# Norms, layer norms and residual sums of a two-model transformer kernel: VectorE's signals carried by its instructions, and one rounding moved to ScalarE

## The reference

```
# first block, each of two layers (x: 512 tokens, s_c: 256 context tokens)
hx = rms_norm(x, norm1_g) * (1 + mod[1]) + mod[0]
x  = x + mod[2] * mixer(hx)                       # mLSTM + convolution, then attention
x  = x + mod[5] * sqrelu_mlp(rms_norm(x, norm2_g) * (1 + mod[4]) + mod[3])

# second block, each of two layers
h = x @ w_in                                      # queries, keys, values and gates of 3 branches
merged = (g[:, :, 0] * (o_mla  @ wb[:MLA_OUT]) + g[:, :, 1] * (o_diff @ wb[MLA_OUT:...])
          + g[:, :, 2] * (o_mem @ wb[...:]))      # g = sigmoid(gates)
x = layernorm(ALPHA * x + merged @ w_out, ln1_g, ln1_b)
f = square(relu(x @ mlp_w1)) @ mlp_w2
x = layernorm(ALPHA * x + f, ln2_g, ln2_b)
```

## Time and profile before

| | |
|---|---|
| time, median of 3 runs | 4470.93 us (4465.73 to 4476.07) |
| time of the profiled execution | 4468.7 us |
| its span, first to last instruction | 4465.8 us |
| mean granted TensorE clock | 0.939 |
| PE busy | 4019.3 us, 90% |
| DVE busy | 2118.9 us, 47% |
| ACT busy | 1495.7 us, 33% |
| POOL busy | 1641.7 us, 37% |

### The profile page before, as it was taken

The page is one execution under the profiler, slowest core; times in us unless marked ns, Lnnn a source line. Parts: engine busy times, 40 slices in busy tenths (PEclk is TensorE's granted clock), DMA queues, the critical chain, the costliest instruction groups (busy, mean ns, idle before and its releaser), DMA issues.

```text
span 4465.8 us, 62758 instructions
## 1 busy us (share of the span) xinstructions
PE 4019.3 (90%) x20662; PEld 3353.9 (75%) x20662; DVE 2118.9 (47%) x3412; ACT 1495.7 (33%) x2419; POOL 1641.7 (37%) x2044
## 2 busy tenths in 40 slices
PE   4887788999988888999999999899988999998997
PEld 3776677999987766888777678688866767876885
DVE  5455464333245776334655632533357376235235
ACT  3111122111124553222545543222236355323223
POOL 0111112333331103666333345356632433544564
PEclk6888898999998999999999999899989999998998
DMA  3232211111111001222211122222211211222222
GB/s 138 101 122 98 106 62 43 62 62 62 63 55 34 20 15 55 97 96 94 67 57 62 53 76 91 71 85 96 97 64 37 76 53 53 96 84 67 98 94 85
DMA packets 92786, 328.64 MB, mean 74 GB/s; under 512 B 10240, under 2 KB 12544, under 8 KB 92544
## 3 DMA queue, kind: packets, MB, share of 16 engines
q1 hardware_dynamic: 90928, 323.61, 21.8%
q10 hardware_dynamic: 1616, 1.90, 0.1%
HBM read 323.38 MB, written 2.10 MB: 73 GB/s over the span
## 4 chain that ended last, share of the span: by engine, by line
issue 67%; POOL 33%; POOLq 1%
POOL Wl L264 33%; POOLq L259 0%; POOLq L261 0%; POOLq L264 0%; POOLq L147 0%; POOLq L258 0%; POOLq L3288 0%
## 5 line engine op out<-in xcount | busy, mean ns | idle before, releaser
L264 POOL TENSOR_TENSOR Wl<-raw,Wh 128x256 fp32r<-128x256 f32 x2040 | 1641.5, 835 | 2823.5 <-ACT Wh L371 2823.4
L371 ACT ACTIVATE Wh<-raw 128x1024 fp32r<-128x1024 f32 x510 | 540.2, 1059 | 1924.1 <-PE psum L1095 1684.6
L1093 PE MATMUL psum<-Hh,Wh 128*128 128x512 f32 (+1 forms) x2704 | 1052.8, 389 | 95.7 <-DVEq L1945 59.9
L1094 PE MATMUL psum<-Hl,Wh 128*128 128x512 f32 (+1 forms) x2704 | 1026.3, 380 | 0.0
L1095 PE MATMUL psum<-Hh,Wl 128*128 128x512 f32 (+1 forms) x2704 | 1025.4, 379 | 0.0
L1093 PE MATMUL psum<-Gh,Wh 128*128 128x512 f32 (+3 forms) x2032 | 756.0, 372 | 31.3 <-DVEq L1945 27.5
L1095 PE MATMUL psum<-Gh,Wl 128*128 128x512 f32 (+3 forms) x2032 | 747.6, 368 | 0.0
L1094 PE MATMUL psum<-Gl,Wh 128*128 128x512 f32 (+3 forms) x2032 | 747.0, 368 | 0.0
L1093 PEld LDWEIGHTS psum<-Hh,Wh 128*128 128x128 f32 x2704 | 525.2, 194 | 230.2 <-DVEq L1945 67.1
L1095 PEld LDWEIGHTS psum<-Hh,Wl 128*128 128x128 f32 x2704 | 525.1, 194 | 72.4
L1094 PEld LDWEIGHTS psum<-Hl,Wh 128*128 128x128 f32 x2704 | 527.1, 195 | 66.0 <-issue 1.3
(11 more groups left out here) (336 smaller groups left out, 4740.2 us busy)
## 6 DMA issues: line engine op xcount, KB each, us to landing
raw<-in_wstream SPq DMA_DIRECT2D x510, 512.0 KB, 3.3
stage<-in_ada SPq DMA_DIRECT2D x80, 512.0 KB, 4.1
M<-in_ada SPq DMA_DIRECT2D x16, 512.0 KB, 4.7
X<-in_xT SPq DMA_DIRECT2D x1, 2048.0 KB, 12.8
out<-X SPq DMA_DIRECT2D x8, 256.0 KB, 2.0
X<-in_ctxT SPq DMA_DIRECT2D x1, 1024.0 KB, 7.8
M<-in_memT ACTq DMA_DIRECT2D x1, 1024.0 KB, 6.1
M<-in_axial ACTq DMA_DIRECT2D x1, 512.0 KB, 3.5
```

The source lines that it names most:

```text
L264: last = pool.tensor_tensor(Wl[:, s, c], raw[:, s, c], Wh[:, s, c].bitcast(F32), ALU.subtract)
L371: act.activation(Wh[:, s], raw[:, s], ACT.Copy).then_inc(v["w_high"], 1)
L1093: pe.matmul(dst, a[0], b[0], start=first, stop=False)
L1094: pe.matmul(dst, a[0], b[1], start=False, stop=False)
```

## The change

1. **Signals by the instruction.** In `rms` the two pieces of `T(k)`, and the two of `Hl(k)`, follow each other without a wait; the signal to ScalarE is raised by the last piece of `T(k)` itself. In `layer_norm` `T(k)` raises `for_act` and `Hl(k)` raises `for_pe` itself (all but the last), with no wait on the chain behind them. In `centred_sums` the subtraction of the early mean raises `for_act` itself. In `add_gated` the addition raises `bank_free` itself, except where the sum is read next (`followed=True`), where nothing changes but the call. In `hidden` the signal to TensorE stands ahead of the one that gives ScalarE's slot back.
2. **The sum of branches.** ScalarE rounds `M` to `Gh` (`high_sums`), VectorE only subtracts (`low_sums`) and signals TensorE by the subtraction itself. Rows 4 and 5 are done inside the third branch, between its steps m = 4 and m = 6; the other six behind it. The projection takes the rows in the order 4, 5, 0, 1, 2, 3, 6, 7 for its first and all further tiles.

```diff
+OUT_ORDER = (4, 5, 0, 1, 2, 3, 6, 7)
...
@@ ScalarE, second_act @@
+    def high_sums(ms):
+
+        act.wait_ge(v["for_act"], wants.next())
+        for m in ms:
+            act.activation(v["Gh"][:, m, X0:TOK], v["M"][:, m * SEQ:(m + 1) * SEQ], ACT.Copy).then_inc(v["high_done"], 1)
+
     def branch(i, paired, begun):
 
         for m in range(0, KT, 2):
+            if i == 2 and m == 6:
+                high_sums(OUT_ORDER[:2])
             if m or not begun:
...
     branch(2, True, True)
+    high_sums(OUT_ORDER[2:])
...
@@ TensorE @@
-                project(w, slice(0, P), G, X0, SEQ, per_k=1 if m == 0 else 0)
+                project(w, slice(0, P), G, X0, SEQ, per_k=1 if m == 0 else 0, ks=OUT_ORDER)
...
@@ VectorE, rms @@
-                        stt(T[k % 3][:, lo:hi], X[:, k, lo:hi], A[:, 8 * c + k:8 * c + k + 1], psum[:, 5 - c, 0:hi - lo],
-                            ALU.mult, ALU.mult)
-                    for_act()
+                        last = dve.scalar_tensor_tensor(out=T[k % 3][:, lo:hi], in0=X[:, k, lo:hi], scalar=A[:, 8 * c + k:8 * c + k + 1],
+                                                        in1=psum[:, 5 - c, 0:hi - lo], op0=ALU.mult, op1=ALU.mult)
+                    last.then_inc(v["for_act"], 1)
...
+                        last = dve.scalar_tensor_tensor(out=Hl[:, k - 2, lo:hi], in0=T[(k - 2) % 3][:, lo:hi],
+                                                        scalar=mod[:, 6 * layer + shift, k - 2, c:c + 1],
+                                                        in1=Hh[:, k - 2, lo:hi].bitcast(F32), op0=ALU.add, op1=ALU.subtract)
+                    do(last)
                     for_pe()
...
@@ VectorE, centred_sums @@
-                tt(x(k), x(k), psum[:, 5, :], ALU.subtract)
-                for_act()
+                dve.tensor_tensor(x(k), x(k), psum[:, 5, :], ALU.subtract).then_inc(v["for_act"], 1)
...
@@ VectorE, layer_norm @@
-                    stt(T[k % 4], x(k), lvec[:, gcol + k:gcol + k + 1], psum[:, 4, :], ALU.mult, ALU.mult)
-                    for_act()
+                    dve.scalar_tensor_tensor(out=T[k % 4], in0=x(k), scalar=lvec[:, gcol + k:gcol + k + 1], in1=psum[:, 4, :],
+                                             op0=ALU.mult, op1=ALU.mult).then_inc(v["for_act"], 1)
...
+                    if k < KT + 1:
+                        last.then_inc(v["for_pe"], 1)
+                    else:
+                        do(last)
+                        for_pe()
...
@@ VectorE, add_gated @@
+                if followed and t0 + n == TOK:
+                    do(last)
+                    free(b)
+                else:
+                    last.then_inc(v["bank_free"][b], 1)
...
@@ VectorE, hidden @@
-                    split(Gh[:, m, t0:t0 + w], Gl[:, m, t0:t0 + w], r)
+                    cp(Gh[:, m, t0:t0 + w], r)
+                    do(dve.tensor_tensor(Gl[:, m, t0:t0 + w], r, Gh[:, m, t0:t0 + w].bitcast(F32), ALU.subtract))
+                    for_pe()
                     give_back()
-                    for_pe()
...
@@ VectorE, sum of branches @@
+            def low_sums(ms):
+
+                for m in ms:
+                    dve.wait_ge(v["high_done"], diff_counts.high_done.next())
+                    dve.tensor_tensor(Gl[:, m, X0:TOK], M[:, m * SEQ:(m + 1) * SEQ], Gh[:, m, X0:TOK].bitcast(F32),
+                                      ALU.subtract).then_inc(v["for_pe"], 1)
+
...
+                    if n == 2 and m == 4:
+                        for_act()
+                        low_sums(OUT_ORDER[:2])
...
-            for m in range(KT):
-                split(Gh[:, m, X0:TOK], Gl[:, m, X0:TOK], M[:, m * SEQ:(m + 1) * SEQ])
-                for_pe()
+            for_act()
+            low_sums(OUT_ORDER[2:])
```

More of the change, by code:

```diff
@@ L585, in _ @@
         act.sem_inc(v["exps_done"], 2)
-        with loop(2, SECOND_TILES, 162, 192 - 104 - 10, 18 + 2 * KT, 0, diff_counts.per_layer("act")) as l:
+        with loop(2, SECOND_TILES, 162, 192 - 104 - 10, 18 + 2 * KT + 2, 0, diff_counts.per_layer("act")) as l:
             act.wait_ge(v["layer_used"], 1 + l)
@@ L2069, in layer_norm, with add_gated @@
                         dve.wait_ge(v["spread_done"], spread.next())
[L2070 to L2071 removed]
+                    dve.scalar_tensor_tensor(out=T[k % 4], in0=x(k), scalar=lvec[:, gcol + k:gcol + k + 1], in1=psum[:, 4, :],
+                                             op0=ALU.mult, op1=ALU.mult).then_inc(v["for_act"], 1)
                 if k > 1:
                     dve.wait_ge(v["handed"], took.next())
[L2074 to L2078 removed]
+                    last = dve.scalar_tensor_tensor(out=Hl[:, k - 2, X0:TOK], in0=T[(k - 2) % 4], scalar=lvec[:, bcol + k - 2:bcol + k - 1],
+                                                    in1=Hh[:, k - 2, X0:TOK].bitcast(F32), op0=ALU.add, op1=ALU.subtract)
+                    if k < KT + 1:
[3 more added lines that the diff above has]
+                        for_pe()
+        def add_gated(m, segs, part, followed=False):
             for t0, n in segs:
@@ L2082, in add_gated @@
                 if part is None:
-                    stt(X[:, m, t0:t0 + n], X[:, m, t0:t0 + n], 1.0, psum[:, b, 0:n], ALU.mult, ALU.add)
+                    last = dve.scalar_tensor_tensor(out=X[:, m, t0:t0 + n], in0=X[:, m, t0:t0 + n], scalar=1.0, in1=psum[:, b, 0:n],
+                                                    op0=ALU.mult, op1=ALU.add)
                 else:
                     for lo, hi, c in parts_of(t0, n):
-                        stt(X[:, m, lo:hi], psum[:, b, lo - t0:hi - t0], mod[:, part, m, c:c + 1], X[:, m, lo:hi],
-                            ALU.mult, ALU.add)
-                free(b)
+                        last = dve.scalar_tensor_tensor(out=X[:, m, lo:hi], in0=psum[:, b, lo - t0:hi - t0], scalar=mod[:, part, m, c:c + 1],
+                                                        in1=X[:, m, lo:hi], op0=ALU.mult, op1=ALU.add)
+                if followed and t0 + n == TOK:
[3 more added lines that the diff above has]
+                    last.then_inc(v["bank_free"][b], 1)
         def add_gated_squared(segs, part, beside=None):
             for m in range(KT):
-                add_gated(m, segs, part)
+                add_gated(m, segs, part, followed=True)
                 for_act()
@@ L2419, in _ @@
         for m in range(KT):
-            add_gated(m, X_SEGS, 6 + 5)
+            add_gated(m, X_SEGS, 6 + 5, followed=True)
             split(Hh[:, m, X0:TOK], Hl[:, m, X0:TOK], X[:, m, X0:TOK])
@@ L2538, in _ @@
             for m in range(KT):
-                add_gated(m, X_SEGS, None)
+                add_gated(m, X_SEGS, None, followed=True)
                 centred_sums(m)
```

8 lines of the change are left out of this document (1 added, 7 removed).

## The result

| | before | changed |
|---|---|---|
| time, median of 4 runs on one chip | 4469.75 us (4465.73 to 4476.07) | 4420.49 us (4416.31 to 4424.55) |
| ratio, 95% interval | | 0.9888 (0.9874 to 0.9902) |
| time of the profiled execution, its span | 4468.7, 4465.8 us | 4416.31, 4414.2 us |
| mean granted TensorE clock | 0.939 | 0.945 |

The change made the kernel 1.1% faster; 4424.0 us were predicted, with a range of 4408 to 4441. In a later comparison, on the chip of the last experiments, the ratio was 0.9906 (0.9892 to 0.9920).

A forecast was written before the change was run, and what follows sets the result against it. TensorE, busy nearly everywhere, waits mostly for VectorE's signals (87.4 us in 55 waits). Terms 15.5 + 7.4 + 13.0 + 10.4 + 0.4 = 46.7 us off 4468.7 give 4422.0; predicted median 4424 us, range 4408 to 4441.

The forecast's parts named there:

- The overlap: VectorE instructions with no wait between them: each starts 0.09 us before the one ahead has ended, bounded 0 to 0.09.
- Rivals 1 and 2: VectorE: 1, no overlap of instructions, 4438 us, 11 in 100; 2, pipe must empty regardless, 4460 us, 4 in 100.
- rival 5: T's remaining waits: a satisfied wait costs the full gap, A and C keep half, about 4437 us; chance within rival 1's.
- A: Layer norm loops: removed gaps plus overlap save 4.1 us in three norms, 3.2 in the last, 15.5 us together.
- rival 3: Behind the norms' restarts: shorter stalls also remove half-rate clock stretches, up to 14 us more, 4410 us; 12 in 100.
- B: Layer norm heads: six gaps from subtraction to S1 save 0.31 us each, 1.9 us a head, 7.4 us for four.
- C: Rms norm loops: removed waits and overlaps save 3.7 us in three norms, 1.9 in the 512-token one, 13.0 us together.
- D: Sum of branches before w_out: ScalarE rounding and two early rows save 5.2 us a layer, 10.4 us.
- D's price: Third branch: ScalarE waits for for_act ahead of a gate's weights; 2.2 us are over, so it costs nothing.
- E: The rest: in hidden TensorE's signal comes one signal earlier, 0.1 us in four handovers, 0.4 us.
- The clock: First tiles behind seven norms: longer half rate after restarts takes the whole gain, 4480 us; 3 in 100 (rival 4).
- One sign against the forecast: Behind the norms: the forecast is wrong if the granted clock stays at 0.5 for more than 4 us.

The follow-up runs named there:

- the pieces' kernel: Kernel before, with only the wait between the two pieces of a row of T and of Hl removed from the rms loop, signals kept: 4463.13 us, ratio 0.9978.
- B alone: Kernel before, with only the layer norm heads changed (subtraction of the early mean raises for_act itself): 4471.63 us, ratio 0.9995.
- D alone: Kernel before, with only the sum of branches changed (ScalarE rounds, VectorE subtracts, two rows early, new row order): 4462.19 us, ratio 0.9979.
- the alone runs: Kernel before with one part of the change each; the rms loops alone, run twice: 4452.05 us (0.9950) and 4457.05 us (0.9967).

## Why the prediction was right, and where its terms were off

- **The overlap** (0.09 us from four instructions of 350 ns) was right in kind and size for forms twice as long, with two tensors in: 0.08 to 0.09. Rivals 1 and 2 are out by the pieces' kernel, and rival 5 by `Hl`, whose own wait costs nothing.
- **A, 15.5 us**: 17.1. The step came at 2.04 for 2.06. The excess is in the first norm, where 4.1 us became 5.7 in the changed kernel: 17 matmuls ran at a pitch of 0.43 us from the loop's start on before and 7 after. So rival 3 was partly true there, by up to 1.6 us; the earlier trace rows had shown the stretch, and I had left it out of the sum. The loop's own edit need not be its cause: B alone and D alone, which leave this loop as it was, won 0.9 and 0.8 us in it.
- **B, 7.4 us**: 3.7. This term was mis-sized. I took the additions to `S1` at their old length and only removed the gap. They compete with GpSimd, and a gap that goes while the other engine is at work is partly filled by waiting for it: 0.90 became 1.21. The sum closes: six gaps gone are 1.9 us a head, the seven additions of the first head grew from 5.35 to 6.65 us, and the square of `X` beside them shrank from 1.15 to 0.69, which leaves 1.0 to 1.1, as measured (1.09). The row stood there: the additions of 0.90 and 0.79 against 0.69 for the same form should have been asked about, and so should the 1.15 for another with two SBUF inputs, before:

```profile
2869.61 1.15 DVE L1902 TENSOR_TENSOR S<-S,X 128x512 f32<-128x512 f32 x1
```

- **C, 13.0 us**: 15.1. The step is 2.34 for 2.36. The first norm (5.4) and the third (4.3) hold the excess, the second (3.5) is under the 3.7; of the first, 0.6 to 0.8 us came in kernels without the edit too, and the alone runs scatter in the same places, so the rest is put down to where the half rate fell, without a run that shows it. The term itself was added up short: 1.8 removed and 23 overlaps of 0.09 are 3.9 a norm, not 3.7. The changed kernel's timeline in the second norm:

```profile
756.84 1.14 DVE L2013 SCALAR_TENSOR_TENSOR Hl<-M,mod,Hh 128x256 fp32r<-128x256 f32 x2
758.12 1.14 DVE L2007 SCALAR_TENSOR_TENSOR M<-X,sc,psum 128x256 f32<-128x256 f32 x2
759.18 1.14 DVE L2013 SCALAR_TENSOR_TENSOR Hl<-M,mod,Hh 128x256 fp32r<-128x256 f32 x2
```

- **D, 10.4 us**: 9.7. The tile takes 9.76 us for the 8.5 said, 14.64 before for the 14.4. The 8.5 went with the 5.9 us of a full-rate tile, while the sum had taken 5.2; 4.9 were measured. The subtractions are slower than taken and the roundings faster; the instructions of line 2524 around that tile (count, shortest/median/longest ns), and ScalarE's roundings there:

```profile
L2524 DVE TENSOR_TENSOR Gl<-M,Gh x6: 679/732/1219, 2803.8 to 2808.0; 128x512 fp32r<-128x512 f32 x6
```

```profile
2803.16 3.23 ACT L610 ACTIVATE Gh<-M 128x512 fp32r<-128x512 f32 x6 [0.73 <-DVEq L1958]
```

  Six roundings in 3.23 us are one every 0.52 (0.63 for the last). The six subtractions run from 2803.8 to 2808.7, 4.9 us, where I had one of 1.09 and five of 0.6, 4.1 in all: two of them take 1.22 us beside GpSimd, which works until 2806.34, and I had counted one. The sum came near since the stall was 2.06 instead of 2.6 us. D's price was nil as said: the two early roundings end at 2787.96, and the weights behind them start 2.5 us later, when TensorE is done with the slot:

```profile
2786.81 1.15 ACT L610 ACTIVATE Gh<-M 128x512 fp32r<-128x512 f32 x2 [0.81 <-DVEq L1958]
2790.45 1.06 ACT L372 ACTIVATE Wh<-raw 128x1024 fp32r<-128x1024 f32 x1 [2.49 <-PE psum L1105]
```

- **E, 0.4 us**: 0.3, as said.
- **The clock** did not take the gain (rival 4): from the start of the loops on, 17, 10 and 17 matmuls at a pitch of 0.43 us before became 7, 9 and 14 in the three layer norms that feed TensorE. One sign against the forecast did come: behind the last restart of the third of them the granted clock stayed at half for 4.7 us, over the 4 us named, where the first had 1.6 and the second 2.2. Part of the closeness of 4424.0 to 4420.49 is luck: B is 3.7 us short, A and C are 3.7 over, and 5.7 us came from stretches that the change leaves alone, which the second comparison (0.9906, 42.4 us less by the medians) does not bear out.

## What to carry to other kernels

Where one engine feeds a waiting TensorE, count the waits on itself that it asks for without need: here each was worth 0.12 us between neighbours and 0.2 to 0.3 with a signal of its own, and the 158 places of A, B and C made 35.9 us, 0.8%. Before pricing a gap, look whether the instruction behind it is already longer than its form elsewhere: then another engine is in its way, and the gap is partly that engine's to give. Where the parts are below the scatter of the runs, align the two traces by matmul number.

## What was not expected of the hardware

- A VectorE instruction whose wait was met 1.8 us before starts 0.08 us before the end of the one ahead, as if it had none; right behind the instruction that meets it the gap is 0.03.
- VectorE's additions with two SBUF inputs took 1.08 to 1.21 us while GpSimd worked and 0.69 us while it was idle, or with one input in PSUM; GpSimd's own took up to 1.19 instead of 0.73 us. One that had begun 0.1 us before GpSimd (2847.59) kept its 0.69, and GpSimd's first took 1.18.
- ScalarE's plain rounding of 128x512 from SBUF to SBUF takes 0.63 us, one every 0.52 us in a row of six, less than the 0.72 of the form with a bias.
- Short waits of up to 0.4 us left the granted clock at 1.00; in the same tile a wait of 2.06 us was followed by matmuls at half rate. A wait of 2.9 us in the MLP was followed by them in one case of three.
